# Rounding each weight tile in two halves of its columns

## What is computed

```python
for i in range(DEPTH):                      # 4 layers; mixers a, b, c, a
    h = mixer_a / mixer_b / mixer_c (x, ...)   # windowed, dilated, block attention
    x = layer_norm(DN_ALPHA * x + h, ln_g[i, 0], ln_b[i, 0])
    x = layer_norm(DN_ALPHA * x + swiglu(x, w_gate_up[i], w_down[i]), ln_g[i, 1], ln_b[i, 1])
...
for layer in range(DEPTH_2):                # 2 layers
    proj = rmsnorm(x, attn_norm_g[layer]) @ w_in[layer]
    # y_a: gated spatial mix; y_b: state space scan with head decays;
    # y_c: differential attention, q and k under rmsnorm per head
    merged = g0 * (y_a @ w_branch_a) + g1 * (y_b @ w_branch_b) + g2 * (y_c @ w_branch_c)
    x = x + merged @ w_out[layer]
    x = x + (silu(gate) * val) @ ffn_w_down[layer]   # gate, val: short convolution of rmsnorm(x) @ w_up
```

## Time and profile before

| | |
|---|---|
| runs | 2438.31, 2438.33, 2441.66 us; median 2438.33 |
| profiled execution | span 2439.8 us from the first to the last instruction |
| TensorE busy | 2337.8 us, 96% of the span |
| VectorE busy | 1511.8 us, 62%; of it low parts 839.8 us |
| ScalarE busy | 1258.7 us, 52%; of it high parts 689.4 us |
| GpSimd busy | 329.5 us, 14% |
| mean granted TensorE clock | 0.988 of full speed |

### The profile page before, as it was taken

How to read it: one execution, slowest core, us unless ns; L and a number is a source line. 1 busy time by engine, 2 the same in 40 slices (tenths; PEclk the granted TensorE clock), 3 DMA queues, 4 the chain that set the end, 5 groups by cost and what they waited for, 6 DMA issues and landing times.

```text
span 2439.8 us, 36757 instructions
## 1 busy us (share of the span) xinstructions
PE 2337.8 (96%) x15344; PEld 2088.2 (86%) x15344; DVE 1511.8 (62%) x2421; ACT 1258.7 (52%) x1792; POOL 329.5 (14%) x307
## 2 busy tenths in 40 slices
PE   7999999998999999999999979989999999899999
PEld 6799888787899778998789968889899898898998
DVE  6754555555744647547765477555777675566875
ACT  5544365554544455444544456464555575554654
POOL 0100022212100313001010003323000023430000
PEclk9999999999999999999999989999999999999999
DMA  6255443332555434555255534334455443334553
GB/s 256 100 202 188 183 158 139 136 125 100 185 187 189 183 120 165 189 190 203 87 190 190 190 137 158 121 121 174 173 189 189 167 180 123 130 147 173 186 188 128
DMA packets 58182, 398.94 MB, mean 164 GB/s; under 512 B 6816, under 2 KB 7072, under 8 KB 11680
## 3 DMA queue, kind: packets, MB, share of 16 engines
q1 hardware_dynamic: 56864, 393.75, 44.2%
q10 hardware_dynamic: 1152, 2.83, 0.3%
HBM read 395.51 MB, written 1.05 MB: 163 GB/s over the span
## 4 chain that ended last, share of the span: by engine, by line
PE 61%; DVE 7%; ACT 4%; issue 2%; POOL 2%; DVEq 0%; ACTq 0%; POOLq 0%
PE b L1166 12%; PE b L1168 11%; PE b L1167 11%; PE b L1099 7%; PE b L1100 7%; PE b L1101 7%; PE b L1104 4%; PE b L1108 2%; ACT whi L1463 2%; DVE wlo L1805 1%; DVE b L1830 1%; POOL xn L2501 1%; DVE st L1892 1%; DVE b L1889 0%; DVE xn L1904 0%
## 5 line engine op out<-in xcount | busy, mean ns | idle before, releaser
L1805 DVE TENSOR_TENSOR wlo<-raw,whi 128x2048 fp32r<-128x2048 f32 x362 | 839.8, 2326 | 497.3 <-ACT whi L1463 496.8
L1463 ACT ACTIVATE whi<-raw 128x2048 fp32r<-128x2048 f32 x362 | 689.4, 1911 | 450.5 <-PE b L1168 246.3
L1166 PE MATMUL b<-xh,whi 128*128 128x256 f32 x2560 | 726.5, 284 | 1.0 <-ACT PT L1463 1.0
L1168 PE MATMUL b<-xh,wlo 128*128 128x256 f32 x2560 | 714.4, 279 | 0.0
L1167 PE MATMUL b<-xl,whi 128*128 128x256 f32 x2560 | 713.9, 279 | 0.0
L1166 PEld LDWEIGHTS b<-xh,whi 128*128 128x128 f32 x2560 | 483.2, 189 | 6.8 <-issue 4.7
L1167 PEld LDWEIGHTS b<-xl,whi 128*128 128x128 f32 x2560 | 484.1, 189 | 1.9
L1168 PEld LDWEIGHTS b<-xh,wlo 128*128 128x128 f32 x2560 | 483.6, 189 | 0.0
L1099 PE MATMUL b<-whi,xh 128*128 128x512 f32 x832 | 342.7, 412 | 31.8 <-DVE xl L1838 16.3
L1100 PE MATMUL b<-wlo,xh 128*128 128x512 f32 x832 | 328.2, 394 | 0.0
L1101 PE MATMUL b<-whi,xl 128*128 128x512 f32 x832 | 328.0, 394 | 0.0
(11 more groups left out here) (228 smaller groups left out, 2626.7 us busy)
## 6 DMA issues: line engine op xcount, KB each, us to landing
raw<-in_w SPq DMA_DIRECT2D x362, 1024.0 KB, 4.8
gt<-in_rows SPq DMA_DIRECT2D x8, 512.0 KB, 4.1
bt<-in_rows SPq DMA_DIRECT2D x8, 512.0 KB, 5.0
abq<-in_rows ACTq DMA_DIRECT2D x2, 768.0 KB, 5.9
x<-in_x SPq DMA_DIRECT2D x1, 1024.0 KB, 6.3
bc<-in_rows SPq DMA_DIRECT2D x4, 256.0 KB, 4.9
out<-x SPq DMA_DIRECT2D x4, 256.0 KB, 2.3
msk<-in_masks SPq DMA_DIRECT2D x1, 768.0 KB, 6.4
```

Source lines behind the costliest of these rows:

```text
L1166: pe.matmul(out, wh[:, k, cs], ah[:, kk, :], start=kk == 0 and s == 0, stop=False, skip_group_check=True)
L1168: last = pe.matmul(out, wl[:, k, cs], ah[:, kk, :], start=False, stop=final and k == 3, skip_group_check=True)
L1463: return ac.activation(out, i, ACT.Copy)
L1805: ve.tensor_tensor(B.wlo[r][:, :], B.raw[r][:, :], B.whi[s][:, :], ALU.subtract).then_inc(sem["loV"], 1)
```

## The change

Both roundings of a tile are issued as two operations of 1024 columns each, part 0 and part 1. `pump` puts in part 0 where it put in the whole, and part 1 at its next call (`halve_part`, `low_part`); only then is the counter set back. Where a tile is forced, or at the end of a block, the parts that are left are put in together. The low part of half p waits for the high part of half p alone; TensorE still waits for the whole tile. The number of columns rounded is the same.

```diff
--- before.py
+++ after.py
@@ -179,6 +179,7 @@
         self.loaded = self.halved = self.used = 0
         self.lows = []
         self.lowtick = self.hightick = 0
+        self.hi_part = 0
         self.closing = False
         self.low_on = {}
         self.freed = set(range(-NHL, 0))
@@ -211,15 +212,38 @@
 
     def halve_next(self):
         if self.halved < NT:
-            self.step("hi", self.halved)
-            self.lows.append(self.halved)
+            for part in range(self.hi_part, 2):
+                self.step("hi", self.halved, part)
+            self.hi_part = 0
+            self.lows.append((self.halved, 0))
             self.halved += 1
 
+    def halve_part(self):
+        if self.hi_part:
+            self.halve_next()
+        else:
+            self.step("hi", self.halved, 0)
+            self.hi_part = 1
+
     def low_now(self, on="V"):
-        i = self.lows.pop(0)
+        i, first = self.lows.pop(0)
+        if first:
+            on = "V"
         self.low_on[i] = on
         self.counts("lo" + on, i)
-        self.step("lo" + on, i)
+        if on == "G":
+            self.step("loG", i)
+            return
+        for part in range(first, 2):
+            self.step("loV", i, part)
+
+    def low_part(self):
+        i, first = self.lows[0]
+        if first:
+            self.low_now()
+        else:
+            self.step("loV", i, 0)
+            self.lows[0] = (i, 1)
 
     def tile(self, want):
         i = self.used
@@ -227,7 +251,7 @@
         self.used += 1
         while self.halved <= i:
             self.halve_next()
-        while self.lows and self.lows[0] <= i:
+        while self.lows and self.lows[0][0] <= i:
             self.low_now()
         return i
 
@@ -245,7 +269,7 @@
         self.hightick = 0
 
     def may_halve(self):
-        return self.halved < min(self.used + NHL - 1, NT) and self.halved - NHL in self.freed
+        return self.hi_part or self.halved < min(self.used + NHL - 1, NT) and self.halved - NHL in self.freed
 
 
 
@@ -256,13 +280,13 @@
     def pump(self, n=1):
         if self.lows and not self.late and not self.closing:
             self.lowtick += 1
-            if self.lowtick >= 2:
-                self.low_now()
+            if self.lowtick >= 2 or self.lows[0][1]:
+                self.low_part()
                 self.lowtick = 0
         if self.may_halve() and not self.late and not self.closing:
             self.hightick += 1
-            if self.hightick >= 2:
-                self.halve_next()
+            if self.hightick >= 2 or self.hi_part:
+                self.halve_part()
                 self.hightick = 0
         if self.pre and next(self.pre[0], "end") == "end":
             self.pre.pop(0)
@@ -1467,12 +1491,12 @@
         ac.dma_start(B.col[:, :], ins["cols"]).then_inc(sem["cols"], 16)
         ac.dma_start(B.posi[:, :], ins["positions"]).then_inc(sem["pos"], 16)
 
-    def hi(i):
-        s, r = i % NHL, i % NRAW
+    def hi(i, part):
+        s, r, cs = i % NHL, i % NRAW, slice(1024 * part, 1024 * part + 1024)
         a.wait_ge(f"w{r}", 16 * (i // NRAW + 1))
         if i >= NHL:
             a.wait_ge(*o.gone[i - NHL])
-        copy(B.whi[s][:, :], B.raw[r][:, :]).then_inc(sem["hi"], 1)
+        copy(B.whi[s][:, cs], B.raw[r][:, cs]).then_inc(sem["hi"], 1)
 
     def turn_x(t, q):
         b, n = use["turned", 0, t, q]
@@ -1799,10 +1823,12 @@
         ve.memset(B.eps[:, 0:1], LN_EPS).then_inc(sem["eps"], 1)
         ve.memset(B.eps[:, 1:2], RMS_EPS).then_inc(sem["eps"], 1)
 
-    def lo(i):
-        s, r = i % NHL, i % NRAW
-        v.wait_ge("hi", i + 1)
-        ve.tensor_tensor(B.wlo[r][:, :], B.raw[r][:, :], B.whi[s][:, :], ALU.subtract).then_inc(sem["loV"], 1)
+    def lo(i, part):
+        s, r, cs = i % NHL, i % NRAW, slice(1024 * part, 1024 * part + 1024)
+        v.wait_ge("hi", 2 * i + part + 1)
+        last = ve.tensor_tensor(B.wlo[r][:, cs], B.raw[r][:, cs], B.whi[s][:, cs], ALU.subtract)
+        if part:
+            last.then_inc(sem["loV"], 1)
 
     def turn_x(t, q):
         b, n = use["turned", 0, t, q]
@@ -2354,7 +2380,7 @@
 
     def lo(i):
         s, r = i % NHL, i % NRAW
-        g.wait_ge("hi", i + 1)
+        g.wait_ge("hi", 2 * i + 2)
         ge.tensor_tensor(B.wlo[r][:, :], B.raw[r][:, :], B.whi[s][:, :], ALU.subtract).then_inc(sem["loG"], 1)
 
     def scale_gb(a):

```

## The result

The changed kernel is slower: 2448.67 us (median of 7 runs, 2444.41 to 2452.34) against 2438.6 (7 runs of the kernel before), a ratio of 1.004 with a 95% interval of 1.0029 to 1.005. That is 10.1 us more; the forecast was 3.4 more.

The account below looks back on a forecast made before the run. TensorE, busy 96% of the span, was taken as the bound, with only its 102 us of waits able to move. Costs of 15.0 less gains of 11.6 gave +3.4 us on 2438.3, so 2441.7; 8-in-10 range 2430 to 2455.

Parts of the forecast that it names:

- rival A: Slower by clock dips at blocks 1, 3, 5, 7 and late tiles: 2448 to 2458 us, middle 2450; chance 0.22.
- block 9's end: Blocks 8, 9 and 10 were to come out within 0.3 us either way, -0.3 in the sum.
- Cost of a half: Two halves cost 0.07 us more than a whole on VectorE, 0.1 to 0.2 on ScalarE, mostly in idle time.
- terms 1, 2: Ends of blocks 2 and 4: +6.9 us, clock dips +3.4; FFN ends +2.1, blocks 0 and 6 +0.3.
- tile 169: Its low part waits behind the rotation, so two halves end after TensorE wants the tile: +1.5 us.
- the decay matmuls: Scan of the second model: TensorE's wait, 0.79 us with its restart, goes; -1.6 us for two layers.
- Of the other tiles, the same sum leaves a margin for all but five: Tiles other than 169 get their low parts in time, except five within 0.5 us: +0.2 us in all.
- Term 5: Second model's query and key norms: low parts leave urgent places, 1.75 and 0.6 us earlier; -4.7 us for two.
- Terms 4 and 7: First-model attention: two halves ahead of `opart` +0.9; shorter blocking -2.4. Also FFN starts -1.5, kernel start -0.8, y transposes -0.6.
- Term 4: First attention of mixer b: two halves ahead of `opart` on VectorE delay freeing a bank TensorE waits for, +0.9 us.
- C: Slower by fixed cost: late rounding makes TensorE wait inside the FFNs, 20 us, 2460 or more; chance 0.08.
- B: Faster: slack behind additions or shorter blocking, low halves following high halves, gives -8.3 us, 2430; chance 0.20.

Follow-up runs that it names:

- e1: The pairs: changed kernel with both halves back to back where the whole stood, in the order and counters of the kernel before; 2434.95 us, 0.9983 of before.
- e5: The running counters: changed kernel with each counter set to 1, not 0, after part 1; 2430.71 us, 0.9962 of the kernel before.
- e7: Changed kernel edited so only high parts are two halves back to back, low parts whole and waiting for both; 2441.99 us, 1.0008 of the kernel before.
- e8: Changed kernel edited so only low parts are two halves back to back, both waiting for the whole high part; 2442.66 us, 1.0012 of before.
- e3: Changed kernel with both low and high parts one call earlier (both counters at >= 1); 2476.68 us, 1.0153 of the kernel before.

## Why the prediction was near, and where it was off

The measured 2448.67 lies in the range, 7 us above the forecast of 2441.7, inside what rival A gave (2448 to 2458). The forecast called it no change; it is a loss clear of the 4.9 us. That the sum is only 7 off is partly luck: it left out costs of some 20 us (late tiles 8.8, the scan's states about 4 in each layer, the query norm's lost gain 1.75 twice) and gains of some 10 (the clock at three places, block 9's end). These sums are estimates from the traces, and some of the pieces overlap.

- **Cost of a half, terms 1, 2, and tile 169: right.** 6.81 for 6.86; blocks 2 and 4 +3.0 and +4.8 for 6.9 and a dip each (one dip came, not two, so 7.8 for 10.3); the FFN ends 4 x 0.4 for 2.1; tile 169 a wait of 1.38 for +1.5. The start gave 0.8 and the decay matmuls 0.7 to 0.8 in each layer, as forecast. (Six times 1.14 is 6.84, not the 6.86 of the sum.)
- **"Of the other tiles, the same sum leaves a margin for all but five": wrong, the first of the steps that failed.** +0.2 was forecast; the seven other waits for low parts sum to 10.4 - 1.4 = 9.0 us. The sum took 1.14 us for a half everywhere. At the four largest (tiles 230, 239 and their likes in the second layer) GpSimd works beside: two halves from 1603.63 took 3.57 us and three from 1680.19 took 6.08, which is 1.8 to 2.0 each.
- **States of the scan: left out of the sum.** +3.3, with the decay's -0.8 in it, and about the same in the second layer, from GpSimd's stretched chain (about 1.5), its later start (about 1.0) and the lower clock behind the wait.
- **Term 5, query norm: VectorE's part right within 0.02 us, the end wrong.** -1.75 was forecast for TensorE and 0 came, since the low parts that left the place ahead of the scaling ran beside GpSimd's rotation. The key's 1.25 us of wait did go, but mostly because TensorE now stands 1.97 us ahead of it for the low part of tile 230: over both waits it gains 0.4, where 0.6 was forecast.
- **Terms 4 and 7: their named places right, the rest of layer 1's attention left out.** Term 4 gave +1.2 for +0.9 (the wait at 457.30 is 1.41 us where it was 0.22). The largest piece of term 7 came as said, in layer 2: the wait of 1.60 us at 878.29 is 0.74 now. But layer 1's attention, where only term 4 and small gains were forecast, took +3.3. It is made of two new waits of 1.03 us (411.52 and 557.68), term 4's 1.2, and the clock: 1.6 gained behind 457, some 2.4 lost between 592 and 606, where it is 0.64 against 0.88 before; a shorter wait at 598.76 gives 0.9 back. That pairs give -1.4 in this stretch and running counters -2.6 (with a clock of 1.00 over 588 to 608) shows that the restart goes with the loss, not how.
- **Clock: half of the term came.** Two dips were priced at the ends of blocks 2 and 4; one came. Dips that went, and new ones elsewhere, had no term. Their balance over the trace is nothing.
- **Block 9's end: wrong.** Within 0.3 was forecast; TensorE's wait fell from 2.65 to 1.11 us, while the low part that stood ahead of `hlo` there went, and with it the 2.90 us in which VectorE waited for a high part.
- **Rivals.** A named late tiles and clock at the FFN ends: the tiles came, more of them than A said; the clock stayed at 1.00 behind three of the four ends (waits of 1.19 us) and was lower only behind the last, where it had been low before (0.53 against 0.62 over 18 us). C, waits inside the FFNs, didn't come. B's mechanism, a low half that follows its high half, is what e1 points to, with 3.9 us at most. In the changed kernel it can't pay, since VectorE hardly waits for high parts there (41 us). The Trainium skill has both sides of this in one section (Perfetto Trace Analysis, "Optimizing Scalar/DVE Operations"): group operations where an engine is saturated, and break them up where an unsaturated one causes bubbles elsewhere. The prediction cited the first; the second fits these runs better: the pieces gain 3.9 us in e1 and 8.6 in e5.

The cause of the loss is shown: two lines that set a counter to 0 and not to 1. With them at most one high part is made in the four calls of a tile where two fitted, so a delay in rounding isn't caught up. They are worth 18.7 us: -8.6 with them at 1 (e5), +10.1 with them at 0. Against wholes, the halves gain 3.9 us in the order of before; in the late order and in that of e5 the difference is 15 and 20, but there the wholes also start one call later.

## What to carry to other kernels

When an operation is cut in two, count what the cut does to the schedule's rate and lead before you price the pieces: here the pieces with the rate kept gain 9 us, and the restarted counters lose 19 against that. A producer and a consumer that are both cut can overlap within one tile; cutting only one of them gained nothing (e7, e8). A dip of the clock in one trace is no gain or loss until the mean over the execution says so. And an operation moved earlier on an in-order engine needs its input there already, or it blocks what stands behind it (e3, 38 us).

## What was not expected of the hardware

Behind a wait of 3.30 us TensorE's granted clock was 1.00 at one block end and 0.51 at another, two blocks on, with the same operations. Behind waits of 2.6 to 2.8 us at block 9's end it was 0.72 over 6 us before and 1.00 in e7 and e8. GpSimd's operation over 64 columns took 0.31 to 0.32 us alone and 1.30 beside VectorE's halves, while the halves went from 1.14 to between 1.8 and 2.0 us.
